# Third MoE of a two-block transformer: the extra expert slots as two strips of 32 per half of the experts, two weight tiles' strips multiplied at once

## The reference

```python
def hierarchical_moe(h, w_rg, b_rg, w_re, b_re, w_gate, w_up, w_down):
    g_prob = jax.nn.softmax((t @ w_rg + b_rg).astype(f32), axis=-1)
    g_p, g_idx = lax.top_k(g_prob, 1)
    ...
    top_l, top_i = lax.top_k(e_in, TOP_K)
    w_k = jax.nn.softmax(top_l, axis=-1) * g_p
    ...
    for e in range(N_EXPERTS):
        hid = jax.nn.silu(t @ w_gate[e]) * (t @ w_up[e])
        out = out + gates[:, e:e + 1] * (hid @ w_down[e])
```

## Time and profile before

| | us |
|---|---|
| median of 3 runs | 1520.02 (1518.67 to 1521.36) |
| profiled execution | 1517.78 |
| its span | 1516.0 |
| PE busy | 1355.5 (89%) |
| VectorE busy | 443.6 (29%) |
| ScalarE busy | 241.5 (16%) |
| GpSimd busy | 102.1 (7%) |
| DMA, mean over the span | 236 GB/s |

### The profile page before, as it was taken

How to read it: one execution, slowest core, us unless ns; L and a number is a source line. 1 busy time by engine, 2 the same in 40 slices (tenths; PEclk the granted TensorE clock), 3 DMA queues, 4 the chain that set the end, 5 groups by cost and what they waited for, 6 DMA issues and landing times.

```text
span 1516.0 us, 18888 instructions
## 1 busy us (share of the span) xinstructions
PE 1355.5 (89%) x7789; PEld 707.7 (47%) x7789; DVE 443.6 (29%) x1252; ACT 241.5 (16%) x595; POOL 102.1 (7%) x195
## 2 busy tenths in 40 slices
PE   3999888999898788979997999979999699999996
PEld 3446544444544555544444874564545333333332
DVE  1104452221303256342224352251114620101113
ACT  0104310111102245101111222011320112000000
POOL 1100000000011000000001000000000111221210
PEclk9999999999999799989999999989999899999998
DMA  8957836999843355439999443365339167999980
GB/s 323 353 153 269 293 111 212 367 344 348 284 166 111 111 206 189 147 115 339 352 334 341 167 158 111 111 226 191 111 111 333 56 218 275 380 387 386 383 326 29
DMA packets 214689, 357.43 MB, mean 236 GB/s; under 512 B 15831, under 2 KB 85904, under 8 KB 214604
## 3 DMA queue, kind: packets, MB, share of 16 engines
q1 hardware_dynamic: 201314, 352.50, 65.6%
q10 hardware_dynamic: 13289, 3.71, 1.1%
HBM read 355.14 MB, written 1.05 MB: 235 GB/s over the span
## 4 chain that ended last, share of the span: by engine, by line
PE 81%; DVE 9%; DMA 4%; issue 2%; ACT 2%; SPq 1%; POOL 0%; DVEq 0%; ACTq 0%; POOLq 0%
PE bank L1941 19%; PE bank L2119 7%; PE bank L2317 6%; PE bank L2145 4%; PE bank L2160 4%; PE bank L2177 4%; PE bank L2556 4%; PE bank L2031 4%; PE bank L1956 3%; PE bank L2379 3%; DMA ring<-in_w_down 3%; PE bank L2605 3%; PE bank L2285 2%; PE bank L2410 2%; PE bank L2327 2%
## 5 line engine op out<-in xcount | busy, mean ns | idle before, releaser
L1941 PE MATMUL bank<-ring,hT 128*128 128x512 f32 x416 | 182.8, 602 | 3.2 <-ACT hT L819 3.0
L1941 PEld LDWEIGHTS bank<-ring,hT 128*128 128x128 f32 x416 | 79.9, 193 | 103.5 <-issue 100.0
L2119 PE MATMUL bank<-ring,A 128*64 128x512 f32 x512 | 113.4, 595 | 6.2 <-issue 3.3
L1941 PE MATMUL bank<-ring,OT 128*128 128x512 f32 x256 | 112.3, 600 | 3.0 <-ACT OT L1089 1.3
L1956 PE MATMUL bank<-ring,cact 128*32 128x128 f32 x2304 | 81.8, 298 | 22.5 <-DMA ring<-in_ada_w 15.2
L2317 PE MATMUL bank<-ring,A 128*64 128x512 f32 x384 | 86.9, 595 | 0.1
L1956 PEld LDWEIGHTS bank<-ring,cact 128*32 128x32 f32 x2304 | 68.3, 120 | 36.2 <-issue 24.3
L692 POOL TENSOR_TENSOR rstd<-rstd,nhalf 128x1 f32<-128x1 f32 x20 | 17.2, 860 | 956.5 <-DVE rstd L1167 956.5
L1941 PEld LDWEIGHTS bank<-ring,OT 128*128 128x128 f32 x256 | 48.9, 193 | 64.0 <-issue 60.3
L2145 PE MATMUL bank<-pb 128*128 128x128 f32 (+1 forms) x512 | 67.9, 288 | 7.7 <-DVE A L1383 5.4
L2145 PEld LDWEIGHTS bank<-pb 128*128 128x128 f32 x512 | 62.9, 200 | 20.2 <-issue 11.4
(11 more groups left out here) (436 smaller groups left out, 1642.2 us busy)
## 6 DMA issues: line engine op xcount, KB each, us to landing
ring<-in_ada_w SPq DMA_DIRECT2D x24, 2048.0 KB, 9.1
ring<-in_moe_w_gate SPq DMA_DIRECT2D x32, 1024.0 KB, 8.0
ring<-in_moe_w_up SPq DMA_DIRECT2D x32, 1024.0 KB, 10.5
ring<-in_moe_w_down SPq DMA_DIRECT2D x16, 2048.0 KB, 12.9
ring<-in_w_gate SPq DMA_DIRECT2D x16, 2048.0 KB, 12.8
ring<-in_w_up SPq DMA_DIRECT2D x16, 2048.0 KB, 13.5
ring<-in_w_down SPq DMA_DIRECT2D x16, 2048.0 KB, 20.8
ring<-in_w_in SPq DMA_DIRECT2D x13, 2048.0 KB, 12.8
```

The lines of the kernel that those rows point to most:

```text
L1941: ins = mm(B[2 * (m % 2) + tt][:], lhs[:, c, tt * P:(tt + 1) * P], w[:, c, :], start=c == 0, stop=c == C - 1)
L2119: ins = mm(B[4][n * b:n * (b + 1), :], h3[:, c, n * b:n * (b + 1)], wv[b][:, :, c, :], start=c == 0, stop=c == C - 1)
```

## The change

Each half of the experts now has two strips of 32 extra slots instead of two sets of 64. The first strip goes to the first expert above 64 tokens; if that expert has more than 96, the second strip is its continuation, otherwise another expert's. So there are 128 extra slots instead of 256, and `gather_more` streams half the columns.

An even tile makes no extra product. Behind an odd tile's main products PE makes four of 32 columns: two strips against the even tile's copied blocks and two against the odd tile's, in the four column quarters of the array and the four partition quarters of bank 4. The rows 64 to 127 hold the odd tiles' part of the sum over c, so VectorE has to add both halves of the bank (`strips_sum`, `hidden`) before the activation and before the product; in the down stage the scatter's matrix has the strips twice (`more_w`), so that it adds them. PE now waits for the copied blocks before the last main pair, an even tile counts as used when its main products are done, and GpSimd waits for PE only in front of even tiles.

```diff
-    more_h = [[Pm_flat[:, P * c:P * (c + 1)] for c in range(6)] + ...
+    more_h = ([cols[:, P * c:P * (c + 1)] for c in range(3)] + ...
-    more_sel = pb[:, :, 2 * D:2 * D + T]
+    more_sel = pb[:, :, 2 * D:2 * D + P]
...
-            if i >= 2:
-                pool.wait_ge(tile_used, n - 1)
+            if i >= 2 and i % 2 == 0:
+                pool.wait_ge(tile_used, n)
...
-            step(v.scalar_tensor_tensor(by_half("first"), picks_of(0), 999.0, by_half("key"), ALU.mult, ALU.add))
+            step(v.tensor_tensor(by_half("first"), picks_of(0), by_half("count"), ALU.mult))
+            step(v.tensor_reduce(low[:, 2, :], by_half("first"), AX.X, ALU.add))
+            step(v.tensor_scalar(low[:, 3, :], low[:, 2, :], 96.0, None, ALU.is_gt))
+            step(v.tensor_scalar(low[:, 4, :], low[:, 3, :], -999.0, 999.0, ALU.mult, ALU.add))
+            step(v.tensor_tensor(by_half("first"), picks_of(0), bc(low[:, 4, :], 2, [P, 2, 8]), ALU.mult))
+            step(v.tensor_tensor(by_half("first"), by_half("first"), by_half("key"), ALU.add))
...
             for tt in range(TT):
-                v.tensor_tensor(more_sel[:, tt].rearrange("p (o k) -> p o k", k=64),
-                                bc(more["place"][:, tt], 2, [P, 2 * NO, 64]), bc(slot_no[:, 0:64], 1, [P, 2 * NO, 64]),
+                second = more["place"][:, tt].rearrange("p (h o) -> p h o", o=NO)[:, :, 1]
+                ins = v.scalar_tensor_tensor(second, low[:, 3, :], -32.0, second, ALU.mult, ALU.add)
+            step(ins)
+            for tt in range(TT):
+                v.tensor_tensor(more_sel[:, tt].rearrange("p (o k) -> p o k", k=32),
+                                bc(more["place"][:, tt], 2, [P, 2 * NO, 32]), bc(slot_no[:, 0:32], 1, [P, 2 * NO, 32]),
                                 ALU.is_equal).then_inc(s["more_selected"], 1)
...
+            def strips_sum(half):
+                tile_ready(dve, n0 + 16 * half + 7)
+                strips = rows_h[4][0:64, :]
+                step(v.tensor_copy(strips, B[4][64:128, :]))
+                v.tensor_tensor(strips, strips, B[4][0:64, :], ALU.add).then_inc(s["strips_summed"], 1)
...
+                strips = rows_h[4][0:64, :]
+                step(v.tensor_copy(strips_up, B[4][64:128, :]))
+                step(v.tensor_tensor(strips_up, strips_up, B[4][0:64, :], ALU.add))
+                v.tensor_tensor(strips, strips, strips_up, ALU.mult).then_inc(s["wide_hid"], 1)
...
-                    ins = mm(B[7][:, 0:T], xn[:, tt, c * P:(c + 1) * P], more_sel[:, tt, :],
+                    ins = mm(B[7][:, 0:P], xn[:, tt, c * P:(c + 1) * P], more_sel[:, tt, :],
...
+                    if r == NR - 1:
+                        pe.wait_ge(s["picked"], n - n0 + 1)
...
+                    elif r == NR - 1 and c % 2 == 0:
+                        ins.then_inc(tile_used, 1)
-                pe.wait_ge(s["picked"], n - n0 + 1)
-                for o in range(NO):
-                    ins = mm(B[4][64 * o:64 * (o + 1), :], more_h[half][c][:, 64 * o:64 * (o + 1)],
-                             picked[(n - n0) % 2][o], start=c == 0, stop=c == C - 1)
-                ins.then_inc(tile_used, 1)
+                if c % 2:
...
+                    for odd in range(2):
+                        for o in range(NO):
+                            row = 64 * odd + 32 * o
+                            ins = mm(B[4][row:row + 32, :], more_h[c - 1 + odd][:, 64 * half + 32 * o:64 * half + 32 * (o + 1)],
+                                     picked[odd][o], start=c == 1, stop=c == C - 1, skip_group_check=True)
+                    ins.then_inc(tile_used, 1)
```

More of the change, by code:

```diff
@@ L943, in wide_act @@
                     act.wait_ge(s["more_gathered"], c + 1)
[L944 to L947, removed]
+                    a.activation(more_h[c], B[7][:, 0:P], ACT.Identity, bias=modc[:, shift, c:c + 1],
+                                 scale=modc[:, scale, c:c + 1]).then_inc(s["more_h_act"], 1)
             def silu(half):
@@ L1445, in moe_rest_dve @@
             large = name == "moe2"
[L1446 removed]
+            masked = 1
             over = overflows(dve, name)
             with dve.If(over > 0):
[L1449 to L1465 removed]
+                if large:
+                    ins = v.tensor_tensor(chosen[:], place[:], bc(more["held"], 1, [P, TT, 16]), ALU.is_gt)
+                else:
+                    ins = v.tensor_scalar(chosen[:].rearrange("p a e -> p (a e)"),
+                                          place[:].rearrange("p a e -> p (a e)"), float(n), None, ALU.is_gt)
+                ins.then_inc(s[f"rest_step{i}"], 1)
+                dve.wait_ge(s[f"rest_step{i}"], 1)
                 v.tensor_tensor(comb[:], comb[:], chosen[:], ALU.mult).then_inc(s[f"rest_hid{i}"], 1)
@@ L1612, in wide_experts @@
                 turned(g)
+            strips_sum(1)
             hidden(1)
@@ L2382, in down @@
                         ins.then_inc(s["wide_down"], 1)
-                if k == 0:
-                    if q == 0:
+                    elif r == NR - 1 and k % 2 == 0:
+                        ins.then_inc(tile_used, 1)
+                if k % 2:
+                    if k == 1 and q == 0:
                         pe.wait_ge(s["wide_hid"], 10)
-                    else:
+                    elif k == 1:
                         pe.wait_ge(s["wide_out_act"], 3 * q)
-                pe.wait_ge(s["picked"], n - n0 + 1)
-                for o in range(NO):
-                    ins = mm(B[4][64 * o:64 * (o + 1), :], hidT_more[half][:, P * k + 64 * o:P * k + 64 * (o + 1)],
-                             picked[(n - n0) % 2][o], start=k == 0, stop=k == 3)
-                ins.then_inc(tile_used, 1)
+                    for odd in range(2):
+                        for o in range(NO):
+                            row, col0 = 64 * odd + 32 * o, 64 * (k - 1 + odd) + 32 * o
+                            ins = mm(B[4][row:row + 32, :], hidT_more[half][:, col0:col0 + 32], picked[odd][o],
+                                     start=k == 1, stop=k == 3, skip_group_check=True)
+                    ins.then_inc(tile_used, 1)
             def scatter(q):
```

74 lines of the change are left out of this document (41 added, 33 removed).

## The result

| | before | after |
|---|---|---|
| median of the first comparison | 1520.02 us | 1504.74 us (1504.24 to 1509.22, 5 runs) |
| profiled execution, span | 1517.78, 1516.0 us | 1504.74, 1502.9 us |
| ratio of the runs, 95% interval | | 0.9921, 0.9896 to 0.9946 |
| second comparison, later | 1518.33 us (1516.09 to 1522.76, 11 runs) | 1507.59 us (1503.56 to 1510.29, 6 runs) |
| its ratio, 95% interval | | 0.9923, 0.9902 to 0.9944 |

The kernel is faster, by some 12 us (the intervals hold 8 to 16) where 8.65 were forecast.

The account below looks back on a forecast made before the run. TensorE bounds the third MoE until the DMA saturates (about tile 12), then transfers at 5.42 us per tile, then TensorE from tile 36. Train 5.4 + end 3.25 = 8.65 us, median 1511.4 us, range 1508 to 1515.5.

Parts of the forecast that it names:

- The frame: Third MoE: savings count before transfers saturate (about tile 12) and after the last transfer wait (tile 36), nothing between.
- The train: Saturated weight transfers from tiles 6 and 7 done to tile 36's landing: moves 5.4 us earlier, bounds 4.5 and 6.3.
- the change of width: TensorE switching between 64- and 32-column products: 0.15 us each, two per group or one before gather or scatter; bounds 0 and 0.4.
- The end stretch: From tile 36 on: 12 extra products become 6 groups, saving 3.25 us, bounds 1.7 and 5.15.
- Group price: Four 32-column extra products side by side on TensorE: 0.90 us per group, bounds 0.86 and 1.08.
- VectorE's chain: Small more_slots steps before the evacuation gather(1) awaits: 1.04 us longer, just hidden; bounds 0 and 0.3.
- The total: Whole kernel: 5.4 + 3.25 = 8.65 us saved, median after 1511.4 us.
- A: Rival, extra products: the four don't run side by side; two at once 1518.7 us (chance 0.03), none 1534 (0.05).
- B: Rival, tiles 25 to 36: TensorE's clock falls in longer waits, loses 3 us, giving 1514; chance 0.08.
- C: Rival, third MoE: as forecast but groups cost 0.86 and switches nothing, 11.4 us gained, 1508.6; chance 0.12.
- D: Rival, weight transfers: train doesn't move, ceiling elsewhere (engine skew or ln2 rows); only 3.3 us gained, 1516.8; chance 0.06.

Follow-up runs that it names:

- the third execution of this code: Changed kernel with groups of four doubled in tiles 36 to 47, its code unchanged up to tile 36: first gathering product to tile 36 took 205.97 us.
- Doubled groups: Changed kernel with every group of four extra products made twice, in tiles 8 to 31, 0 to 7 or 36 to 47: ratios to before 0.9935, 0.9955, 0.9974.
- the late rows: Changed kernel with the two 0.5 MB ln2 rows requested after the down stage's third quarter, not after tile 31: ratios to before 0.9917 and 0.9908.
- tiles 8 to 31 doubled: Changed kernel with every group of four extra products made twice in tiles 8 to 31: ratio to before 0.9935 (0.9910 to 0.9959).

## Why the prediction was right, and where its size was off

**The frame held.** Saving counts before the train closes and behind tile 36, and nowhere between. 10.3 us of work added between changed nothing; 5.15 added behind came out whole. Added ahead, 3.4 and 3.3 were seen in full when tile 7 was done, and at tile 36 as 2.1 to 3.2 and 1.6 to 2.7. TensorE met the DMA at tile 25 and last waited at tile 36, as forecast.

**The train was mis-sized**: 5.4 us forecast, 213.26 - 206.82 = 6.4 measured (means of two profiles each; the first pair alone gives 7.0, and with the 205.97 of the third execution of this code it is 6.7). That is above the upper bound of 6.3, which let the prices of the group and the changes of width vary, and not that of gather_more; the lower bound, by the forecast's own prices, would be 4.7 and not 4.5. Tile 7 was done 6.25 us earlier (5.6 forecast) and tile 6 5.98 (5.4 forecast: before 1271.06 - 1201.32 = 69.74; after 1258.95 + 3.58 - 1198.77 = 63.76). Two prices were wrong, both too dear. gather_more costs 0.45 and not 0.50, so it saves 0.41 each: I priced it by L2145, a chain of 16. And a group costs 1.00 with the change of width ahead of it, where I had 0.90 + 0.15: a pair saves 2 x 0.86 - 1.00 = 0.72, not 0.67. 8 x 0.41 + 4 x 0.72 = 6.2 for tile 7, and 7 x 0.41 + 3 x 0.72 + 0.86 = 5.9 for tile 6. What tile 36 moved beyond tile 6's 5.98, 0.4 us, is no more than the spread of the train between executions (0.6 before, 1.1 after), and I give it no cause.

**The end stretch was nearly right**: 3.57 for 3.25. Doubled groups take 1.85 and single ones 1.00, so a group is 0.86 and the change of width ahead of it 0.14; the change behind it is in the next main products, 7.02 for two tiles where 2 x 3.43 = 6.86 stood before. That is the 0.30 per group that I had. With 0.86 for 0.90 the sum becomes 3.25 + 6 x 0.04 = 3.5.

**Group price.** Of the bounds 0.86 and 1.08 the lower one was right. The 26% that 32-column quarters showed at L1956 with 128 moving columns is not there with 512. Neither did the fixed cost of 0.027 us per pass show that the forecast leaned to: it gave 0.91, and doubling a group added 0.86. What makes L1956 dearer stays open.

**VectorE's chain** ended where forecast: hidden with nothing to spare, 1204.90 against 1204.90. In executions with a shorter first gather it was not hidden and cost 0.07 to 0.36 us, where the bounds were 0 and 0.3.

**The total.** 6.4 + 3.57 = 10.0 us in the third MoE. The timed difference is about 12, with 8 to 16 allowed. The first median, 1504.74, lay below the range because both went one way: the term above by 1.3 us, and the runs, with a mean granted clock of 0.9632 against 0.9622 in the second comparison, worth 0.9 us by the estimate above; the run of 1504.74 itself had 0.966, where the profiled 1517.78 of before had 0.964. I took the range from the unknown prices and gave the kernel's own spread no part in it, though three runs of before already spanned 2.7 us and later ones 1511.6 to 1526.4. The timed ratios of the experiments on the changed kernel, the late rows aside, stand 1 to 4 us further from that of the changed kernel than the traces do. In part that is the lower clock of their runs, 1.0 to 1.8 us for three of them by the table at equal clock. The rest lies with the changed kernel, whose own times gained more than its traces, and that is not explained.

**The rivals.** A (the four products queue) is refuted by the rows of the group, 0.86 for four. B (the clock falls in the waits) is refuted: 1.00 over 1343 to 1406. C (groups 0.86 and switches nothing, 11.4 us) was half right, in the group's price; the change of width is not free. With gather_more at 0.45 it would have given more still. D (the train doesn't move) is refuted in its main part: the train moved by more than 5.4. Its doubt about the ln2 rows pointed at something real, a pause of 2.5 us in both kernels; as it is in both, it took nothing from the gain.

## What to carry to other kernels

Find the last wait on a transfer and the point at which the train of transfers closes, and count a saving only outside these two: here 10 us of work inside cost nothing, 5 us behind cost 5, and 3.4 us ahead cost 2 to 3. Small products that fill only part of the array are worth packing four wide even when each streams its own operand; here a group cost one such stream, 0.86 us, plus two changes of width, 0.30 us. And give the range the spread of the kernel's own runs before the unknown prices: here the stretches ahead of the change moved by up to 11 us between executions of the same code.

## What the runs showed of the hardware

- Four fp32 products of 128 rows, 32 columns and 512 moving columns, each with its own moving operand, take 0.86 us together, as two of 64 columns do. A change between 64-column and 32-column products cost 0.14 us going in (1.00 against 0.86) and 0.16 coming out (7.02 against 2 x 3.43).
- 1 MB asked for on ScalarE's queue while the ring's queue ran at 387 GB/s held up one 2 MB tile by some 2.5 us (7.91 to 8.25 between the copies that mark the landings of tiles 32 and 33, instead of 5.42) in nine of the ten executions that asked for it there, and in the tenth (tiles 8 to 31 doubled) some 2.4 us spread over tiles 32 to 34. In both executions with the 1 MB asked for later it was 5.41.
- The start of tile 36, counted from the first gathering product, varied by 0.6 us between two executions of before, by 1.1 among three executions of the changed code, and by 3.0 in the version with the late rows. The end of tile 7 varied by 0.06 and 0.14.
- A run whose mean granted clock was 0.001 lower took 0.9 us longer (122 runs, an estimate by a straight line within each kernel's runs).
- TensorE kept the full clock through 63 us in which it was 78% busy with waits of 0.7 to 1.8 us, while attention stretches at 66% had 1.00 in one execution and 0.66 in another (650 to 665 us, the rows above).
